# The second gate's projection as seven half-size products (Strassen's scheme), with its sums on GpSimd and VectorE, placed ahead of the first branch's products

## What is computed

```python
xn = rms_norm(x, norm1_g)
sq, sk, sv, dq, dk, dv, iq, ik, iw, g_sb, g_dsa = jnp.split(xn @ w_in, IN_SPLITS, axis=-1)
merged = (sigmoid(g_sb) * (o_sb.reshape(B, L, SB_WIDTH) @ w_sb_branch)
          + sigmoid(g_dsa) * (o_dsa.reshape(B, L, DSA_WIDTH) @ w_dsa_branch))
h = x + merged @ w_out
```

## Time and profile before

| | |
|---|---|
| time, median of 3 | 819.17 us (818.43 to 819.59) |
| profiled execution, its own time | 819.9 us |
| its span | 818.0 us |
| TensorE busy | 784.7 us (96%) |
| VectorE, ScalarE, GpSimd busy | 329.5, 228.8, 185.0 us |
| chain that ended last | PE 85%, DMA 5%, SP's queue 4%, DVE 2% |
| TensorE's clock as granted, mean | 0.989 |

### The profile page before, as it was taken

The page is one execution under the profiler, slowest core; times in us unless marked ns, Lnnn a source line. Parts: engine busy times, 40 slices in busy tenths (PEclk is TensorE's granted clock), DMA queues, the critical chain, the costliest instruction groups (busy, mean ns, idle before and its releaser), DMA issues.

```text
span 818.0 us, 11857 instructions
## 1 busy us (share of the span) xinstructions
PE 784.7 (96%) x4615; PEld 492.3 (60%) x4615; DVE 329.5 (40%) x933; ACT 228.8 (28%) x464; POOL 185.0 (23%) x210
## 2 busy tenths in 40 slices
PE   6999999999999999999999999999999999999885
PEld 4465443488767667776677784556655555555552
DVE  5222464899243555565633365435611111111100
ACT  3031233101243544434333522221222222222111
POOL 2315332000023433300000010010233333333322
PEclk9999999999999999999999999999999999999998
DMA  8821302043120200304040399448899999999994
GB/s 263 220 104 51 88 8 97 1 160 116 44 103 2 104 1 1 111 1 155 1 103 1 139 415 365 129 143 279 300 387 395 400 399 398 397 398 395 404 402 139
DMA packets 59816, 155.81 MB, mean 190 GB/s; under 512 B 15688, under 2 KB 22280, under 8 KB 52592
## 3 DMA queue, kind: packets, MB, share of 16 engines
q1 hardware_dynamic: 50848, 141.74, 46.6%
q0 software_dynamic: 8912, 13.32, 6.1%
HBM read 147.38 MB, written 15.99 MB: 200 GB/s over the span
## 4 chain that ended last, share of the span: by engine, by line
PE 85%; DMA 5%; SPq 4%; DVE 2%; ACT 1%; POOL 1%; issue 1%; POOLq 0%; DVEq 0%; ACTq 0%
PE quad L858 19%; PE pair L1175 11%; PE pair L1060 7%; PE quad L1308 7%; PE quad L1428 6%; PE pair L1428 5%; PE quad L932 4%; DMA arena<-in_w_up 3%; PE quad L1443 3%; PE pair L1443 3%; SPq L724 2%; PE pair L848 2%; PE pair L979 2%; SPq L732 1%; PE quad L1080 1%; PE pair L1102 1%
## 5 line engine op out<-in xcount | busy, mean ns | idle before, releaser
L858 PE MATMUL quad<-ring_w,xnT 128*128 128x512 f32 (+1 forms) x192 | 79.3, 553 | 0.0
L1905 POOL TENSOR_TENSOR arena<-arena 128x511 f32<-128x511 f32 (+5 forms) x36 | 35.5, 1007 | 155.1 <-DVE arena L2168 131.7
L1060 PE MATMUL pair<-xnT,ring_w 128*128 128x272 f32 x256 | 67.4, 402 | 0.4 <-ACT tabs L1645 0.4
L1961 POOL DMA_INDIRECT out_y_prompt<-ring_w,idx x32 | 50.7, 1586 | 65.0 <-ACT ring_w L1813 64.4
L1175 PE MATMUL pair<-xnT,ring_w 128*128 128x272 f32 x256 | 64.6, 398 | 0.0
L858 PE MATMUL quad<-xnT,ring_w 128*128 128x280 f32 (+1 forms) x256 | 60.6, 396 | 0.0
L1060 PEld LDWEIGHTS pair<-xnT,ring_w 128*128 128x128 f32 x256 | 45.5, 190 | 15.8 <-issue 7.1
L858 PEld LDWEIGHTS quad<-xnT,ring_w 128*128 128x128 f32 x256 | 48.2, 190 | 10.8 <-issue 0.4
L1956 POOL DMA_INDIRECT ring_w<-xn_d,idx x32 | 33.0, 1032 | 91.8 <-PE pair L1419 45.0
L1175 PEld LDWEIGHTS pair<-xnT,ring_w 128*128 128x128 f32 x256 | 46.5, 190 | 11.5 <-issue 2.7
L858 PEld LDWEIGHTS quad<-ring_w,xnT 128*128 128x128 f32 x192 | 34.3, 189 | 31.7 <-issue 26.0
(11 more groups left out here) (292 smaller groups left out, 1176.0 us busy)
## 6 DMA issues: line engine op xcount, KB each, us to landing
arena<-in_w_gate SPq DMA_DIRECT2D x21, 1024.0 KB
arena<-in_w_up SPq DMA_DIRECT2D x21, 1024.0 KB
arena<-in_w_down SPq DMA_DIRECT2D x40, 512.0 KB
ring_w<-in_w_in SPq DMA_DIRECT2D x8, 2048.0 KB, 9.0
ring_w<-in_w_down SPq DMA_DIRECT2D x20, 512.0 KB
xnT<-in_w_gate SPq DMA_DIRECT2D x4, 1024.0 KB
xnT<-in_w_up SPq DMA_DIRECT2D x4, 1024.0 KB
ring_w<-in_w_in SPq DMA_DIRECT2D x3, 1024.0 KB, 7.7
```

The lines of the kernel that those rows point to most:

```text
L858: last = nc.tensor.matmul(o, l, r, start=i == 0, stop=i == len(mms) - 1)
L1060: last = nc.tensor.matmul(bank[6 + job % 2][:, 0:hi - lo], chunk8(6 + cb // 4)[:, k, c0:c0 + P], xT[:, k, lo:hi], start=k == 0, stop=k == ...
L1905: nc.gpsimd.tensor_tensor(v, v, lb[:, i % LB, u, 1:n], ALU.mult).then_inc(w_ready, 1)
L1961: pool.indirect_dma_start(yp_half, bass.IndirectOffsetOnAxis(ap=rows, axis=0), Yb[:, q, :], None, bounds_check=2 * SEQ - 1, oob_is_err=Fal ...
```

## The change

The second gate's matrix is cut in four quarters, A[i][h]: output half i (chunk 10 + i) by input half h. The transposed activations are cut likewise: `x_part(h, g)`, input half h by row part g. Strassen's scheme in Winograd's form makes the four output quarters from seven products in place of eight. Each product has 4 column blocks c, and each of these is one job of 4 matmuls, so 28 jobs (16 to 43) of 112 matmuls replace 16 jobs of 128. M2, M4 and M3 are added in the bank to M1, M7 and M5, which had just been copied out of it. ScalarE copies M1, M2, M7 and M4 (jobs 16 to 31); VectorE adds M6, M5 and M3 (jobs 32 to 43) to what lies in SBUF (`gate2_summed`), at two places of its step. GpSimd makes four sums of activations (4x272 columns each, into `merged`), sixteen of weights (4x128 each, in place in `ring_w`) and eight of output quarters (272 each). The first branch's product becomes jobs 44 to 59. The plan's fills become (7, 5), (7, 6), (7, 5), (7, 6), (6, 4), (6, 5), (6, 4), (6, 5), (4, 4), (5, 4), (4, 4), (4, 4), (7, 6), then (3, 3) or (4, 3). The order of loads and what some of them wait for changes with it, as does the moment of `residual(0)` and `residual(1)`.

```diff
-A_MMS, G_MMS = 16 * 4, 16 * KT
+GATE2_JOBS = [(m, c) for pair in ((0, 1), (2, 3)) for m in ("M1", "M2") for c in pair]
+GATE2_JOBS += [(m, c) for pair in ((0, 1), (2, 3)) for m in ("M7", "M4") for c in pair]
+GATE2_JOBS += [("M6", c) for c in range(4)]
+GATE2_JOBS += [(m, c) for pair in ((0, 1), (2, 3)) for m in ("M5", "M3") for c in pair]
+NG2 = len(GATE2_JOBS)
+G2_ACT, G2_END = 16 + 16, 16 + NG2
+NBJ = NG2 + 16
...
+A_MMS, G_MMS = 16 * 4, NG2 * 4
...
+def gate2_job(m, c):
+    return 16 + GATE2_JOBS.index((m, c))
...
-        slots = [0, 1, 0, 1, 0, 1, 0, 1, 0, 1, 1, 0]
+        slots = [0, 1, 0, 1, 0, 1, 0, 1, 0, 1, 0, 1]
         chunk_at = [wslot[s] for s in slots] + [xnT[:, 0:4096], wslot[0]]
         pj_used = {0: 5, 1: 10, 2: 15, 3: 20, 4: 28, 5: 36, 9: 52, 12: 64, 13: 65}
-        gd_used = {6: 8, 7: 16, 8: 32, 10: 40, 11: 48}
-        held_by = {2: 0, 3: 1, 4: 2, 5: 3, 6: 4, 7: 5, 8: 6, 10: 7, 11: 8, 9: 10, 12: 11, 13: 11}
+        gd_used = {6: 8, 7: 16, 10: gate2_job("M6", 3) + 1, 11: G2_END, 8: 16 + NBJ}
+        held_by = {2: 0, 3: 1, 4: 2, 5: 3, 6: 4, 7: 5, 10: 6, 11: 7, 8: 10, 9: 11, 12: 11, 13: 8}
...
+            if n == 8:
+                eng.wait_ge(g2_sums_ready, 20)
...
+        gA = [[k_half(chunk_at[10 + i], h) for h in range(2)] for i in range(2)]
+        gT1, gT2, gT3, gT4 = (merged[:, 4 * h:4 * h + 4, lo:hi] for h in range(2) for lo, hi in FG)
+        g2_operands = {"M1": (gA[0][0], x_part(0, 0)), "M2": (gA[0][1], x_part(1, 0)), "M7": (gA[0][0], gT3),
+                       "M4": (gA[1][1], gT4), "M6": (gA[0][0], gT2), "M5": (gA[1][0], gT1), "M3": (gA[1][1], x_part(1, 1))}
+        def quarter(i, g, c):
+            lo, hi = FG[g]
+            return gds[4 * i + c][:, lo:hi]
...
-            for n in (7, 8, 10, 11, 9, 12, 13):
+            for n in (7, 10, 11, 8, 9, 12, 13):
...
+            def bank_emptied(job):
+                if job < G2_ACT:
+                    pe.wait_ge(gd_free, job + 1)
+                elif job < G2_END:
+                    pe.wait_ge(g2_out, job + 1 - G2_ACT)
+                else:
+                    pe.wait_ge(gd_free, job + 1 - (G2_END - G2_ACT))
             def branch_products():
-                for job in range(16, 48):
-                    cb, g = job // 2 % 8, job % 2
+                for job in range(16, G2_END):
+                    m, c = GATE2_JOBS[job - 16]
+                    bank_emptied(job - 2)
+                    if job == 16:
+                        chunk_arrived(pe, 10)
+                    if m == "M7":
+                        pe.wait_ge(g2_sums_ready, 5 + 2 * c)
+                    if m == "M4":
+                        chunk_arrived(pe, 11)
+                    if m == "M6":
+                        pe.wait_ge(g2_sums_ready, 13 + 2 * c)
+                    if m == "M3":
+                        pe.wait_ge(g2_sums_ready, 14 + 2 * c)
+                    w, x = g2_operands[m]
+                    more = m in ("M2", "M4", "M3")
+                    for k in range(4):
+                        last = nc.tensor.matmul(bank[6 + job % 2][:, 0:272], w[:, k, P * c:P * (c + 1)], x[:, k, :],
+                                                start=k == 0 and not more, stop=k == 3, skip_group_check=True)
+                        if k == 3:
+                            last.then_inc(gd_ready, 1)
+                        yield
+                chunk_arrived(pe, 8)
+                for job in range(G2_END, 16 + NBJ):
+                    cb, g = (job - G2_END) // 2, job % 2
                     lo, hi = FG[g]
-                    pe.wait_ge(gd_free, job - 1)
-                    if job == 16:
-                        chunk_arrived(pe, 8)
-                    if job >= 32 and cb % 4 == 0 and g == 0:
-                        chunk_arrived(pe, 10 + cb // 4)
-                    if job < 32:
-                        w, c0, rhs = chunk_at[8].rearrange("p (k c) -> p k c", k=4), P * cb, osbT
-                    else:
-                        w, c0, rhs = chunk8(10 + cb // 4), P * (cb % 4), xT
-                    kt = w.shape[1]
-                    for k in range(kt):
-                        last = nc.tensor.matmul(bank[6 + job % 2][:, 0:hi - lo], w[:, k, c0:c0 + P], rhs[:, k, lo:hi],
-                                                start=k == 0, stop=k == kt - 1)
-                        if k == kt - 1:
+                    bank_emptied(job - 2)
+                    w = chunk_at[8].rearrange("p (k c) -> p k c", k=4)
+                    for k in range(4):
+                        last = nc.tensor.matmul(bank[6 + job % 2][:, 0:hi - lo], w[:, k, P * cb:P * (cb + 1)],
+                                                osbT[:, k, lo:hi], start=k == 0, stop=k == 3)
+                        if k == 3:
...
+                    jobs_copied[0] += 1
+                    if G2_ACT <= job < G2_END:
+                        continue
+                    if job < G2_ACT:
+                        m, c = GATE2_JOBS[job - 16]
+                        dst = {"M1": quarter(0, 1, c), "M2": quarter(0, 0, c), "M7": quarter(1, 1, c), "M4": quarter(1, 0, c)}[m]
+                    else:
+                        lo, hi = FG[job % 2]
+                        dst = merged[:, (job - G2_END) // 2, lo:hi]
                     act.wait_ge(gd_ready, job + 1)
-                    nc.scalar.activation(dst, bank[6 + job % 2][:, 0:hi - lo], ACT.Copy).then_inc(gd_free, 1)
-                    jobs_copied[0] += 1
+                    nc.scalar.activation(dst, bank[6 + job % 2][:, 0:272], ACT.Copy).then_inc(gd_free, 1)
...
-            branches_copied(32)
+            branches_copied(NBJ)
+            act.wait_ge(g2_out, G2_END - G2_ACT)
+            act.wait_ge(g2_u_added, 8)
...
+            def summed(dst, x, y, op, needs=0):
+                if needs:
+                    pool.wait_ge(g2_sums_ready, needs)
+                nc.gpsimd.tensor_tensor(dst, x, y, op).then_inc(g2_sums_ready, 1)
+                g2_sums[0] += 1
+            summed(gT1, x_part(0, 1), x_part(0, 0), ALU.subtract)
+            summed(gT2, x_part(1, 1), gT1, ALU.subtract, 1)
+            summed(gT3, x_part(1, 1), x_part(0, 1), ALU.subtract)
+            summed(gT4, x_part(1, 0), gT2, ALU.subtract, 2)
+            def of_column_block(i, h, c):
+                return gA[i][h][:, :, P * c:P * (c + 1)]
+            def first_weight_sums(c):
+                pool.wait_ge(gd_ready, gate2_job("M1", c) + 1)
+                a11, a21, a22 = (of_column_block(i, h, c) for i, h in ((0, 0), (1, 0), (1, 1)))
+                summed(a11, a11, a21, ALU.subtract)
+                summed(a21, a21, a22, ALU.add, 5 + 2 * c)
+            def last_weight_sums(c):
+                pool.wait_ge(gd_ready, gate2_job("M4", c) + 1)
+                s3, a12, a22 = (of_column_block(i, h, c) for i, h in ((0, 0), (0, 1), (1, 1)))
+                summed(s3, a22, s3, ALU.subtract, 12)
+                summed(a22, a12, s3, ALU.subtract, 13 + 2 * c)
+            chunk_arrived(pool, 10)
+            chunk_arrived(pool, 11)
+            first_weight_sums(0)
+            first_weight_sums(1)
             for h in range(NH):
                 kv = h // 4
                 pool.dma_start(dvM[N_META * h:N_META * (h + 1), h, :], dvP[DEC:DEC + N_META, NT - 1, 64 * kv:64 * kv + 64])\
                     .then_inc(dvm_in, 16)
+            first_weight_sums(2)
+            first_weight_sums(3)
             pool.dma_start(wr[:, :, 0:4], a["w_group"].rearrange("(k p) c -> p k c", p=P)).then_inc(wr_in, 16)
             pool.dma_start(wr[:, :, 4:36], a["w_router"].rearrange("(k p) c -> p k c", p=P)).then_inc(wr_in, 16)
+            for c in range(4):
+                last_weight_sums(c)
+            pool.wait_ge(gd_free, G2_ACT)
+            for c in range(4):
+                pool.wait_ge(g2_out, c + 1)
+                for g in range(2):
+                    v = quarter(1, g, c)
+                    nc.gpsimd.tensor_tensor(v, v, quarter(0, 1, c), ALU.add).then_inc(g2_u_added, 1)
...
-            pool.wait_ge(gd_ready, 32)
+            pool.wait_ge(gd_ready, 16 + NBJ)
             residual(0)
             residual(1)
...
+            def gate2_summed(upto):
+                while g2_summed[0] < min(16 + upto, G2_END):
+                    job = g2_summed[0]
+                    g2_summed[0] += 1
+                    m, c = GATE2_JOBS[job - 16]
+                    dst = quarter(1, 1, c) if m == "M5" else quarter(0, 1, c)
+                    dve.wait_ge(gd_ready, job + 1)
+                    if m != "M6":
+                        dve.wait_ge(g2_u_added, 2 * c + 2)
+                    nc.vector.tensor_tensor(dst, bank[6 + job % 2][:, 0:272], dst, ALU.add).then_inc(g2_out, 1)
             for i, (t, b) in enumerate(DSA_JOBS):
+                gate2_summed(branches_done(i - 1, 2))
                 if i < SAMPLE_JOB:
...
                 nc.vector.sem_inc(lb_ready, 1)
+                gate2_summed(branches_done(i, 1))
```

(28 more changed lines are left out.)

## The result

The changed kernel takes 821.04 us (median of 20 runs, 819.57 to 823.35); the kernel before, in as many runs, 819.41 (817.41 to 822.70). The ratio is 1.002, 95% interval 1.0011 to 1.003: 1.6 us slower, where 816.1 and 3.1 us faster were forecast. The profiled execution took 821.09 us, with a span of 819.2.

What follows compares the result with a forecast made beforehand. TensorE was taken to bound the filler, busy 129.51 of 129.51 us. Terms -7.4 - 0.7 + 5.3 - 0.3 = -3.1 us took the profiled 819.9 to 816.8, the median to 816.1; range 811.0 to 820.0.

Steps and rivals of the forecast that it cites:

- So I cost 28 sums at nothing: GpSimd's sums during the filler: ready before TensorE needs them, slack 4 to 5 us, so no time charged.
- the time is the same by both: GpSimd's sums: at the fast or the slow row's price, some 4 us apart, the kernel's time is unchanged.
- Removed, -7.4 us: TensorE's filler: 176 matmuls in place of 192, 16 fewer at 0.461 us each, 7.4 us less.
- Old waits, -0.7: Filler: TensorE's 0.7 us of waits for ScalarE's copies out of the banks go with the new fills.
- VectorE's waits, 5.3 us in steps 6 to 10: Filler: TensorE waits behind VectorE's line of bank sums, selection and normalisation, 5.3 us in all; bounds nothing to 7.3.
- None before step 5: Filler: TensorE's waits on VectorE, about 5 us, fall in steps 6 to 10, with none before step 5.
- ScalarE nothing: Filler: ScalarE copies 32 jobs as before and adds no wait, also in steps 10 to 17.
- Loads, -0.3: Full DMA stretch after the filler: 1 MB less volume gains between nothing and 0.76 us, taken as 0.3.
- The rest moves as one piece: After the filler: loads and engines follow TensorE's counts, so everything later, experts included, shifts by the same amount.
- Rival 4: Experts: the gain is made and lost again because the DMA engines are full there; 818.9 us, chance 0.07.
- Rival 1: Filler: VectorE never holds TensorE, so its sums cost nothing; 810.8 us, chance 0.16.
- Rival 3: M7's jobs 25, 28, 29: TensorE waits for GpSimd, kernel slower; 821.1 at 1.5 times its prices; chance 0.11.

Runs made afterwards that it cites:

- e1: The changed kernel with GpSimd's 20 sums of activations and weights left out: median 818.56 us, ratio 0.9987, filler stretch 126.86 us.
- e8: The changed kernel with only VectorE's selection moved behind normalisation, reduction and F0's bank sums: ratio 0.9955, filler stretch 125.32 us.
- e6: The changed kernel with activation sums in four pieces and VectorE's selection moved behind normalisation, reduction and F0's bank sums: 811.98 us, ratio 0.9907.
- e4: The kernel before with the changed kernel's order of products, loads and residual rows, but eight products and no sums: ratio 0.9991, filler stretch 129.28 us.
- e3: The changed kernel with M6, M5 and M3 copied by ScalarE, VectorE's additions left out: ratio 0.9966, filler stretch 126.77 us.
- e2: The changed kernel with each of GpSimd's four activation sums cut into four instructions of 272 columns: 816.62 us, ratio 0.9957.
- e9: The changed kernel with only GpSimd's four activation sums left out: ratio 0.998, filler stretch 126.85 us.
- e10: The changed kernel with only GpSimd's sixteen weight sums left out: ratio 0.9976, filler stretch 127.18 us.
- e12: e4 plus eight GpSimd sums that nobody waits for, four of 1088 elements with different operands, four of 512: ratio 0.9997, filler stretch 129.61 us.
- e7: e4 plus four GpSimd sums of 1088 elements, same operand twice, that nobody waits for: ratio 1.0002, filler stretch 129.28 us.

## Why the prediction was wrong, step by step

**The step that failed is "So I cost 28 sums at nothing; TensorE's own matmuls are the cover."** The sums are ready in time, so for TensorE the cover holds. The step asked who waits for the sums; it didn't ask whom they keep waiting. They cost 4.84 us by e1, from 131.70 - 126.86, in the traces, and some 3.7 in the medians. The first 3.2 of it are waits: step 2's scores begin 17.2 us after the filler in the changed kernel and 14.0 in e1 (0.79 and 1.94 idle; the rest, 0.5, I put down to the pipeline that fills again after each). The other 1.6 us go with the slower clock behind them, which e8's trace doesn't have.

The forecast did cite the rule, and read it one way. It weighed whether VectorE slows GpSimd, and found "the time is the same by both". Two rows of its own spoke the other way round: VectorE's line in a step is 6.3 us of some 7.2, and a sum of 2.5 us is longer than what is left. And the mean of 1469 ns hid the hold itself. In the trace of before, of two sums of 511 elements in a row the first begins beside a scan of VectorE's, and the first scan of 384 elements behind them begins beside the second sum; then the same scan with no sum beside it (at 273.19, 275.01, 275.62 and 257.79 us, in the columns of the earlier trace rows):

```profile
L1905 POOL TENSOR_TENSOR arena<-arena 128x511 f32<-128x511 f32 x1 | 1.9, 1855 | 4.7 <-ACT arena L1663 4.7
L1905 POOL TENSOR_TENSOR arena<-arena 128x511 f32<-128x511 f32 x1 | 1.1, 1085 | 0.0
L2168 DVE TENSOR_TENSOR_SCAN arena<-arena,small 128x384 f32<-128x384 f32 x1 | 1.3, 1282 | 0.0
L2168 DVE TENSOR_TENSOR_SCAN arena<-arena,small 128x384 f32<-128x384 f32 x1 | 1.0, 957 | 0.0
```

So 1469 is no slower kind, but a mean of held and free sums, and the hold goes both ways. The Trainium skill has the rule in the form that was needed (SBUF — State Buffer, Who interferes with whom): whichever of the two starts first keeps the shared pair of ports for its whole instruction, and the other is blocked, not slowed; on VectorE it concerns two SBUF inputs (against a GpSimd instruction that reads SBUF) and the two-port modes, which `tensor_scalar` can enter. By that rule, the trace agrees: held are L2363, L2321 (TENSOR_SCALAR) and L2316 (two SBUF inputs); not held are RECIPROCAL (167 ns), the scores' reduction and the bank sums, with one input in a bank (0.71 us and 439 ns), MAX8 and MATCH_REPLACE8 (0.73 and 0.71).

The other steps:

- **Removed, -7.4 us.** Right: 122.12 us in e6.
- **Old waits, -0.7.** They are waits of weight loads, and TensorE's matmuls were busy without a gap. The order alone gives 0.2 (e4), and e6 gives 7.39 for the matmuls and the old waits together. Off by 0.5 to 0.7 us.
- **VectorE's waits, 5.3 us in steps 6 to 10.** Right in mechanism, nearly right in size; e1 against e6 gives 4.74, e3 4.9. The walk said 1.4 for step 6's matmul, 0.7 for step 7's, 1.5 for step 8's transposes, 1.0 for step 10; the changed kernel shows 1.14, 0.61, 1.30 and 0.70. The 0.7 for step 9 doesn't show as idle time at all. The idle sum is 3.75; the other 1.0 of the 4.74 is TensorE's busy time (123.11 us in e1, 122.12 in e6), the refilling after each wait, which the walk didn't price. So the sum came out closer than its parts:

```profile
386.54 0.72 PE L1221 MATMUL pair<-arena,ring_w 128*128 128x272 f32 x2 [1.14 <-DVE arena L2337]
...
395.30 2.10 PE L1221 MATMUL pair<-xnT,ring_w 128*128 128x272 f32 x8 [0.61 <-DVE arena L2337]
...
401.39 0.87 PE L1334 MATMUL pair<-cst,arena 128*128 128x128 f32 x6 [1.30 <-DVE arena L2321]
```

- **"None before step 5".** Wrong: 0.79 and 1.94 us, by VectorE and by ScalarE's copy behind it.
- **ScalarE nothing.** True of its work, and of steps 10 to 17. But its copies stand behind exponentials that wait for VectorE.
- **Loads, -0.3.** From the filler's end to the output stage's L883, 36.51 us against 37.01; over all traces with seven products 36.5 to 36.9, in the two of before 37.0 and 37.2: about -0.4.
- **The rest moves as one piece.** Right: from the first expert to the end 238.4 us against 238.2. Rival 4 is out; e6 kept its 7.4 (7.3 in the medians).
- **Rival 1** (VectorE never holds TensorE, 810.8) is nearly what e6 reaches, by moving the selection. **Rival 3** had the right engine and sign and the wrong mechanism: no TensorE wait on GpSimd exists, and its prices are at the low end.

By terms: -7.39 (matmuls, e6) + 4.74 (VectorE's sums) + 4.84 (GpSimd's hold) = +2.19 on the filler, and +1.6 in the medians. Each term is the difference of two kernels of one chain, so that they add up is no check; that e2, e9, e10 and e3 give 4.84, 4.85, 4.5 and 4.9 for the same two costs is.

Not settled: why the clock fell in the changed kernel and in e3 and not in e8, after nearly the same idle time. With one trace of each kernel it is also open in how many executions it falls; the 1.6 us are not shown for the median.

## What to carry to other kernels

Work put on GpSimd isn't free because it is early: while it runs, look at each VectorE instruction with two SBUF inputs or of a kind such as TENSOR_SCALAR, add to each up to one whole GpSimd instruction, and follow who waits. A group whose single instructions differ by half a us at one shape is the sign; a mean hides it. Keep GpSimd's instructions short beside a chain that VectorE is on, and put VectorE's work that nobody waits for at the end of its step. When jobs are halved, banks come round twice as fast: a copy that was never urgent can become so (here read from the plan and the waits, not varied alone).

## What the runs showed of the hardware that I had not expected

- A VectorE instruction of 170 ns takes up to 1560, one of 192 up to 2410, and ends within 0.05 us of the end of the GpSimd sum that runs. GpSimd's next sum doesn't overtake: VectorE gets its turn after one. GpSimd is held in turn: the weight sum at 339.93 takes 1.46 us in place of 1.27, behind a normalisation that ends at 340.26.
- GpSimd's issuing of small copies can hold VectorE too, but not always: 854 ns in place of 193 for L2316 at 345.46, while in e12 the same instruction beside the same copies takes 192.
- A GpSimd sum of 1088 elements takes 2.49 us with two different inputs (e12) and 2.00 with the same one twice (e7).
- Behind a second idle time of 1.9 us TensorE's granted clock went to 0.81 and then 0.50 (1.2 GHz) until 350 us, which by e8 cost 1.6 us, nearly as much as the idle itself. In another kernel (e8), behind the same two idle times, it stayed at 2.4 GHz.
